# First input projection: sums of products for two pairs of column blocks, and rotary work in earlier steps

## The reference

```python
h = rmsnorm(x, norm_mix[l])
proj = h @ w_in[l]
qa, ka, va, qb, kb, vb, ga, gb = jnp.split(proj, split_points, axis=-1)
qa = rope(rmsnorm(qa.reshape(b, s_len, A_Q_HEADS, HEAD_DIM), a_q_norm[l]), pos)
ka = rope(rmsnorm(ka.reshape(b, s_len, A_KV_HEADS, HEAD_DIM), a_k_norm[l]), pos)
```

## Time and profile before

| | |
|---|---|
| median of 3 runs | 2459.51 us (2459.29 to 2459.89) |
| profiled execution | 2459.43 us |
| its span | 2457.7 us |
| granted TensorE clock, mean | 0.999 |
| TensorE busy | 2445.9 us |
| VectorE busy | 1726.5 us |
| ScalarE busy | 1334.1 us |
| POOL busy | 66.4 us |

### The profile page before, as it was taken

The page is one execution under the profiler, slowest core; times in us unless marked ns, Lnnn a source line. Parts: engine busy times, 40 slices in busy tenths (PEclk is TensorE's granted clock), DMA queues, the critical chain, the costliest instruction groups (busy, mean ns, idle before and its releaser), DMA issues.

```text
span 2457.7 us, 31700 instructions
## 1 busy us (share of the span) xinstructions
PE 2445.9 (100%) x12392; PEld 2072.9 (84%) x12392; DVE 1726.5 (70%) x2077; ACT 1334.1 (54%) x1694; POOL 66.4 (3%) x90
## 2 busy tenths in 40 slices
PE   9999999999999999999999999999999999999998
PEld 7888888888888888888888788888888888888887
DVE  5756767655678777787875457755668779788676
ACT  6444556445555645565555445454656556556453
POOL 0100100000000000000000000000000000000000
PEclk9999999999999999999999999999999999999999
DMA  9655565655555765567557565555565666756663
GB/s 328 206 192 172 164 170 172 224 187 189 189 190 171 244 201 188 188 205 232 181 203 241 163 206 167 163 167 176 171 196 176 220 199 207 220 170 234 216 212 129
DMA packets 256343, 480.98 MB, mean 196 GB/s; under 512 B 23600, under 2 KB 27184, under 8 KB 255584
## 3 DMA queue, kind: packets, MB, share of 16 engines
q1 hardware_dynamic: 251728, 470.98, 57.7%
q0 software_dynamic: 4352, 8.39, 2.0%
q10 hardware_dynamic: 144, 0.03, 0.0%
HBM read 468.85 MB, written 2.13 MB: 192 GB/s over the span
## 4 chain that ended last, share of the span: by engine, by line
PE 98%; DVE 1%; issue 0%; ACT 0%; DMA 0%; DVEq 0%; POOLq 0%; ACTq 0%
PE psum L2364 21%; PE psum L2273 14%; PE psum L2275 14%; PE psum L2274 14%; PE psum L2372 11%; PE psum L2589 4%; PE psum L2591 4%; PE psum L2590 4%; PE psum L2608 2%; PE psum L2609 2%; PE psum L2610 2%; PE psum L2329 1%; PE psum L2334 1%; PE psum L2389 1%; PE psum L2435 0%; DVE wl L1463 0%
## 5 line engine op out<-in xcount | busy, mean ns | idle before, releaser
L1463 DVE TENSOR_TENSOR wl<-raw,wh 128x1024 fp32r<-128x1024 f32 x833 | 1015.3, 1225 | 644.8 <-ACT wh L907 639.8
L907 ACT ACTIVATE wh<-raw 128x1024 fp32r<-128x1024 f32 x833 | 873.3, 1057 | 734.2 <-PE psum L2275 317.1
L2273 PE MATMUL psum<-wh,ha 128*128 128x512 f32 x1248 | 499.4, 400 | 0.7 <-DVE ha L1632 0.7
L2275 PE MATMUL psum<-wh,ha 128*128 128x512 f32 x1248 | 487.1, 390 | 0.0
L2274 PE MATMUL psum<-wl,ha 128*128 128x512 f32 x1248 | 486.5, 390 | 0.0
L2364 PE MATMUL psum<-ha,wh 128*128 128x512 f32 x1344 | 313.1, 390 | 0.0
L2364 PEld LDWEIGHTS psum<-ha,wh 128*128 128x128 f32 x1344 | 249.6, 188 | 50.1
L2275 PEld LDWEIGHTS psum<-wh,ha 128*128 128x128 f32 x1248 | 234.2, 188 | 50.8
L2273 PEld LDWEIGHTS psum<-wh,ha 128*128 128x128 f32 x1248 | 234.6, 188 | 48.3 <-issue 3.3
L2274 PEld LDWEIGHTS psum<-wl,ha 128*128 128x128 f32 x1248 | 234.9, 188 | 44.8
L2364 PE MATMUL psum<-hb,wh 128*128 128x512 f32 x896 | 209.1, 390 | 0.0
(11 more groups left out here) (347 smaller groups left out, 2853.9 us busy)
## 6 DMA issues: line engine op xcount, KB each, us to landing
raw<-in_w_up SPq DMA_DIRECT2D x152, 1024.0 KB, 5.1
raw<-in_w_in SPq DMA_DIRECT2D x116, 1024.0 KB, 5.1
raw<-in_w_down SPq DMA_DIRECT2D x108, 1024.0 KB, 5.1
raw<-in_w_out SPq DMA_DIRECT2D x32, 1024.0 KB, 5.0
raw<-in_w_branch_a SPq DMA_DIRECT2D x8, 1024.0 KB, 5.0
raw<-in_w_branch_b SPq DMA_DIRECT2D x8, 1024.0 KB, 4.9
x_rows<-conv POOLq DMA_DIRECT2D x8, 512.0 KB, 6.6
raw<-in_w_in SPq DMA_DIRECT2D x5, 512.0 KB, 8.0
```

What stands on the lines that cost most here:

```text
L907: act.activation(wh[q % SPLIT_SLOTS][:], src, ACT.Copy).then_inc(hi_done, 1)
L1463: dve.tensor_tensor(wl[q % SPLIT_SLOTS][:], src, wh[q % SPLIT_SLOTS][:].bitcast(F32), ALU.subtract).then_inc(lo_done, 1)
L2273: pe.matmul(acc, hi, wh[s][:, c, :], start=first and c == 0, stop=False)
L2275: ins = pe.matmul(acc, lo, wh[s][:, c, :], start=False, stop=last and c == 1)
```

## The change

Blocks 3 and 4 become a pair, then block 7 runs plainly, blocks 5 and 6 are the second pair, and block 8 runs plainly. In a pair, the weight rows 1024 to 2047 (two of four loads for a block) stay plain, 8 steps of 12 matmuls, and the rows 0 to 1023 become two groups of seven steps of 6 matmuls: 22 steps for 16, and 84 steps for 72 in the stage. The steps of a pair stand in the order of the first 22 steps of `DOWN2_STEPS`, but the sums of the second group begin three steps ahead, not two.

```diff
+IN1_PAIR = [(2, 4), (2, 5), (3, 4), (3, 5)] + seven(1, 0) + [(2, 6), (2, 7)] + seven(1, 1) + [(3, 6), (3, 7)]
+IN1_PAIR_LOADS = [(2, 2), (3, 2), (2, 0), (3, 0), (2, 3), (2, 1), (3, 1), (3, 3)]
+IN1_PAIRS = [(3, 4), (5, 6)]
+S_IN1_PAIR = [24, 24 + len(IN1_PAIR) + 8]
```

VectorE sums the two parts of x and makes four sums for each group in steps 6 and 8, and the low parts of these in steps 7 and 9; ScalarE makes their high parts in its steps 8 and 10, behind its squares of x:

```diff
+            chain.link(dve.tensor_tensor(x_gained[:], both[:, :, 0, :], both[:, :, 1, :], ALU.add))
+            chain.link(dve.tensor_tensor(a_sum0[:, 0], a21, a22, ALU.add))
+            chain.link(dve.tensor_tensor(a_sum0[:, 1], a_sum0[:, 0], a11, ALU.subtract))
+            dve.tensor_tensor(a_sum0[:, 2], a11, a21, ALU.subtract)
+            dve.tensor_tensor(a_sum0[:, 3], a12, a_sum0[:, 1], ALU.subtract).then_inc(sem["x_sums_ok"], 1)
```

The rotary work moves to steps 14 to 37, and the roots on POOL become three instructions of 8 numbers, the mask adds behind the third:

```diff
-            if s == 24:
+            if s == 14:
                 rotation_tables()
...
-            if 26 <= s < 32:
-                if s == 26:
-                    dve.wait_ge(row_free, FREE + 3)
-                piece_sums(s - 26)
...
-            if s in range(36, 54, 3):
-                if s == 36:
-                    dve.wait_ge(sem["an_rs"], 1)
-                piece_rotated((s - 36) // 3)
...
+        piece_steps = {19: 0, 20: 1, 22: 2, 23: 3, 36: 4, 37: 5}
+            if s in (15, 17, 24):
+                i = (15, 17, 24).index(s)
+                dve.wait_ge(row_free, FREE + i + 1)
...
+                piece_sums(2 * i)
+                piece_sums(2 * i + 1)
+                dve.sem_inc(sem["an_ss"], 1)
+            if s in piece_steps:
+                i = piece_steps[s]
+                dve.wait_ge(sem["an_rs"], i // 2 + 1)
+                piece_rotated(i)
+            for i in range(2):
+                n = s - S_IN1_PAIR[i]
+                if 0 <= n < len(IN1_PAIR):
+                    weight_sums(IN1_DOWN + i, n, w_sum0)
+                if 22 <= n < 30:
+                    fold_pair(i, n - 22)
...
-        inverse_root(rsq[:, 0:24], ssq[:, 0:24], 1.0 / HD, 24, sem["an_rs"])
+        for i in range(3):
+            pool.wait_ge(sem["an_ss"], i + 1)
+            inverse_root(rsq[:, 8 * i:8 * i + 8], ssq[:, 8 * i:8 * i + 8], 1.0 / HD, 8, sem["an_rs"])
```

More of the change, by code:

```diff
@@ L59, with seven @@
 T5_BUCKETS = 32
+def seven(pair, group):
+    return [(pair, group, k) for k in range(7)]
+IN1_PAIR = [(2, 4), (2, 5), (3, 4), (3, 5)] + seven(1, 0) + [(2, 6), (2, 7)] + seven(1, 1) + [(3, 6), (3, 7)]
+IN1_PAIR_LOADS = [(2, 2), (3, 2), (2, 0), (3, 0), (2, 3), (2, 1), (3, 1), (3, 3)]
+IN1_PAIRS = [(3, 4), (5, 6)]
+IN1_ORDER = [0, 1, 2, 3, 4, 7, 5, 6, 8]
 S_IN1 = 0
-S_GATE = S_IN1 + 8 * IN1_BLOCKS
+S_IN1_PAIR = [24, 24 + len(IN1_PAIR) + 8]
+L_IN1_PAIR = [12, 12 + 8 + 4]
+S_GATE = S_IN1_PAIR[1] + len(IN1_PAIR) + 8
 S_BRANCH = S_GATE + 8 * GATE_BLOCKS
@@ L84, with early_load @@
 S_IN2 = _s
-L_UP1, L_DOWN1 = [S_FF1 // 2], []
+def early_load(step):
+    extra = len(IN1_PAIR) - 16
+    return (step - extra * sum(step >= s for s in S_IN1_PAIR)) // 2
+L_UP1, L_DOWN1 = [early_load(S_FF1)], []
 for _n in range(2):
@@ L161, in load_done @@
     part = max(p for p in range(3) if p == 0 or u >= L_UP1[p])
-    return (S_UP1[part] if part else 0) + 2 * (u - (L_UP1[part] if part else 0)) + 2
+    if part == 0:
+        return 2 * u + 2 + (len(IN1_PAIR) - 16) * sum(u >= n for n in L_IN1_PAIR)
+    return S_UP1[part] + 2 * (u - L_UP1[part]) + 2
 R_IN1 = 0
@@ L1647, in _, with weight_sum @@
             row_lo(q, 1)
-        for s in range(1, 8 * IN1_BLOCKS):
+        def weight_sum(down, pair, group, n, w_sum):
+            s0, first_load, steps, loads = DOWNS[down]
+            u = first_load + loads.index((2 * pair, group))
+            for v in (u, u + 1):
+                dve.wait_ge(raw_in[v % RAW_SLOTS], 16 * (v // RAW_SLOTS + 1))
+            (b11, b21), (b12, b22) = ([raw[v % RAW_SLOTS][:, 2 * k:2 * k + 2, :] for k in range(2)] for v in (u, u + 1))
+            q = s0 + steps.index((pair, group, 0))
+            made = sums_before(q)
+            if n == 0 and down >= IN1_DOWN and made:
+                dve.wait_ge(lo_done, max(n7 for n7, _, _ in SEVENS if n7 < q) + 7)
+            if n == 2:
+                dve.wait_ge(sem["sum_ok"], made + 1)
+            if n == 3:
+                dve.wait_ge(sem["sum_ok"], made + 3)
+                dve.wait_ge(lo_done, q + 4)
+            plus, minus = ((b12, b11), (b22, b12), (b22, w_sum[0][:]), (b21, w_sum[2][:]))[n]
+            dve.tensor_tensor(w_sum[n % 3][:], plus, minus, ALU.subtract).then_inc(sem["sum_ok"], 1)
@@ new lines, in weight_sums, with x_sums @@
+        def weight_sums(down, s, w_sum):
+            s0, _, steps, _ = DOWNS[down]
+            for n7, step in enumerate(steps):
+                if len(step) == 3 and step[2] == 0:
+                    n = s - sums_begin(steps, step[0], step[1])
+                    if 0 <= n < 4:
+                        weight_sum(down, step[0], step[1], n, w_sum)
+        def x_sums(group):
+            (a11, a12), (a21, a22) = ([x_gained[:, 2 * k:2 * k + 2, P * t:P * t + P] for k in range(2)]
+                                      for t in range(NT))
+            both = ha[:, 4 * group:4 * group + 4, :, :].bitcast(F32)
+            if group:
+                dve.wait_ge(sem["x_sums_hi"], group)
+            chain.link(dve.tensor_tensor(x_gained[:], both[:, :, 0, :], both[:, :, 1, :], ALU.add))
[3 more added lines that the diff above has]
+            dve.tensor_tensor(a_sum0[:, 3], a12, a_sum0[:, 1], ALU.subtract).then_inc(sem["x_sums_ok"], 1)
@@ L1649, in _ @@
+        piece_steps = {19: 0, 20: 1, 22: 2, 23: 3, 36: 4, 37: 5}
+        for s in range(1, S_GATE):
             if s < 5:
@@ L2485, in head_stage, with hb_by, seven_bank, down_banks @@
                 ins.then_inc(sem["at_o"], 1)
+        def hb_by(base, per_count):
+            return lambda j: pe.wait_ge(sem["hb_lo"], base + (2 * j + 1) // 4 + 1)
+        def seven_bank(pair, k):
+            own, shared = 4 * pair, 4 - 4 * pair
+            return (shared, own, own + 2, shared + 1, shared + 3, shared + 2, own + 1)[k]
+        def down_banks(step):
+            if len(step) == 2:
+                return {(step[0] // 2, 2 * step[0] + t) for t in range(NT)}
+            return {(step[0], seven_bank(step[0], step[2]))}
@@ new lines, in down_edges, with down_plain @@
+        def down_edges(steps, s, pair, bank):
+            uses = [n for n, step in enumerate(steps) if (pair, bank) in down_banks(step)]
+            return s == uses[0], s == uses[-1]
+        def down_plain(down, src, acts, s, b, j):
+            q, steps = DOWNS[down][0] + s, DOWNS[down][2]
+            if acts is not None:
+                hb_by(acts, 4)(j)
+            pe.wait_ge(lo_done, q + 1)
+            w = q % SPLIT_SLOTS
+            for c in range(2):
+                for t in range(NT):
+                    acc = psum[:, 2 * b + t, :]
+                    first, last = down_edges(steps, s, b // 2, 2 * b + t)
+                    hi, lo = (src[:, 2 * j + c, part, t * P:(t + 1) * P] for part in range(2))
+                    pe.matmul(acc, hi, wh[w][:, c, :], start=first and c == 0, stop=False)
+                    pe.matmul(acc, hi, wl[w][:, c, :], start=False, stop=False)
+                    ins = pe.matmul(acc, lo, wh[w][:, c, :], start=False, stop=last and c == 1)
+            ins.then_inc(mm_done, 1)
@@ new lines, in down_product @@
+        def down_product(down, src, sums_hi, sums_lo, s, pair, group, k):
+            q, steps = DOWNS[down][0] + s, DOWNS[down][2]
+            pe.wait_ge(lo_done, q + 1)
+            w, bank = q % SPLIT_SLOTS, seven_bank(pair, k)
+            acc = psum[:, bank, :]
+            first, last = down_edges(steps, s, pair, bank)
+            for c in range(2):
+                if k in (0, 1, 6):
+                    t, half = ((0, 0), (0, 1), (1, 1))[(0, 1, 6).index(k)]
+                    hi, lo = (src[:, 4 * group + 2 * half + c, part, P * t:P * t + P] for part in range(2))
+                else:
+                    n = (3, 0, 2, 1)[k - 2]
+                    hi, lo = sums_hi[group][:, n, c, :], sums_lo[group][:, n, c, :]
+                pe.matmul(acc, hi, wh[w][:, c, :], start=first and c == 0, stop=False)
+                pe.matmul(acc, hi, wl[w][:, c, :], start=False, stop=False)
+                ins = pe.matmul(acc, lo, wh[w][:, c, :], start=False, stop=last and c == 1)
+            ins.then_inc(mm_done, 1)
@@ L2573, in down_edges @@
[L2573 to L2592, removed]
```

198 lines of the change are left out of this document (118 added, 80 removed).

## The result

After: 2463.31 us (median of 21 runs, 2462.88 to 2464.90). Before: 2459.51 us (21 runs, 2459.11 to 2459.91). The ratio is 1.0017 [1.0011, 1.0023]: slower, by 3.8 us between the medians, which is clear of no change but less than the 0.2% (4.9 us) set as the bound.

The account below looks back on a forecast made before the run. TensorE bounds the kernel, with VectorE the next limit in groups of seven. Terms -5.4 + 2.0 + 2.5 + 3.1 = +2.2 us on the profiled 2459.43 gave 2461.7 us; range 2457.5 to 2466.0.

Parts of the forecast that it names:

- TensorE, -5.4: First projection: 840 products instead of 864, 24 fewer at 0.2267 us each, all on the path: -5.4 us.
- Sums of x: Steps 6 to 9: VectorE's added sums of x and low parts delay nothing; 0 us, bound 0 to 1.
- First group: Steps 28 to 34, after rotary work: VectorE never idle, step 32's low part late; +2.0 us with restarts, bound 1 to 3.
- Bias adds: POOL's two adds, now amid the first group, take time from VectorE's full queue; +2.5 us, bounds 0 and 2.6.
- Roots: POOL's three roots beside VectorE: 0 by the trace row, about 5.0 us by the skill's rule; the sum took 0.
- Second group: First pair, steps 37 to 43: four sums of weights and two small rotations delay step 41; +3.1 us, bound 2 to 4.
- Second pair, loads, unrolled code: Second pair without rotary work, weight loads, and unrolled code for three engines: 0 us each; bounds to 1, 0.5 and 1.
- the roots hold VectorE too: Slower rival: three POOL roots between steps 15 and 26 delay VectorE, arriving whole at step 32; +5.0, 2466.7 us; chance 0.15.
- the bias adds cost nothing: Rival: POOL waits for a pause or runs after step 32's low part; -0.3 us, 2459.1 us; chance 0.2.
- VectorE keeps pace: Faster rival: less queued between steps 14 and 32, rotations find gaps, the whole 5.4 us stays; 2454.0 us; chance 0.08.

Follow-up runs that it names:

- the version without gaps: Against the kernel after: last four rotations moved to later steps, POOL's bias adds held until the first pair is folded, ScalarE's copy at step 14; 2454.35 us.
- the two-edit version: Against the kernel after: last four rotations moved to later steps and POOL's bias adds held until the first pair is folded, copy left at step 13; 2454.31 us.

## Why the prediction was right, and which term was off

The forecast was 2461.7 us, no difference that can be told: measured 2463.31. The mechanism was the one named, the gain of the products handed back by VectorE, and the gaps stand where the prediction put them: before steps 29 to 32 and 40 to 41, all ended by low parts, none in the second pair. By its steps:

- **TensorE, -5.4:** measured -5.44, and -5.2 net in the version without gaps.
- **Sums of x, 0 (bound 0 to 1): mis-sized.** The run with the copy moved puts 1.3 us on it, more than its bound. The step that failed is "Walked through with ScalarE's order, the low part of step 12 keeps about 0.7 us": that low part did keep its time, but the walk left out the norm's root on POOL and the copy behind it. What the sums of x delayed was not their own low part but ScalarE's squares and POOL's small instructions, and through them the start of step 17's low part, which the next term took at 45.88 "with nothing queued". It began at 47.26.
- **First group, +2.0:** of the 5.55 us of gaps, 2.2 go with the adds and 1.3 with the copy's step; 2.05 are left for the rotary queue, if the parts simply add. With the rotations, the adds and the restarts as counted, the only thing wrong was when the queue began.
- **Bias adds, +2.5 (0 to 2.6):** 2.2 by the stretched rows, and as much by the gaps of the run without them. They began at 84.67, not 81.5, since the last squares came later and the root took 2.49 us, not a third of 5.02, but that is still within the group.
- **Roots, 0 by the row, 5.0 by the rule:** the row was right. The Trainium skill (SBUF — State Buffer, Who interferes with whom) says that a VectorE instruction with two inputs in SBUF contends with a GpSimd instruction that reads SBUF, and that the ports they share are an exclusive lock. For the adds the trace agrees (2.30 us for 1.22). For the roots it doesn't: VectorE lost nothing, while POOL's small instructions waited, 1.29 us for the first of a root, where the one before, begun in a pause of VectorE, took 0.22.
- **Second group, +3.1:** measured 3.05, and 1.6 with one rotation.
- **Second pair, loads, unrolled code, 0:** no gap there, and no gap of after is ended by a load. The load that the prediction gave "about 5.6 us" had cover only because VectorE was late: see the gap behind it in the kernel with the rotations and the adds late. Some 0.45 us of the profiled difference lies outside the counted gaps, 0.2 in remainders within the two groups and 0.25 in later stages; what makes the latter wasn't tried.

The rival "the roots hold VectorE too" gave 2466.7 us and is refuted by the unstretched rows beside a root; "the bias adds cost nothing" by the late adds; "VectorE keeps pace" by the gaps. The last one describes the two-edit version: its 2454.0 us is within 0.4 us of what that measured.

The ends of the range don't follow from the terms that the prediction names for them: without the adds and with the low bound of one group its sum gives about 2458.1, not 2457.5, and with all upper bounds about 2467.2, not 2466.0. The measured time lies inside either.

## What to carry to other kernels

When fewer products make another engine the bound, first list everything that stands in that engine's queue ahead of the dense stretch and on engines that feed it, and move what isn't due there: here four rotations and two adds, none of them due, cost more than the 24 products gave. Work moved ahead of a dense stretch is saved only as far as the relay lets the engine run ahead; if the queue runs empty once on the way, what was saved before that moment is gone. When a sum assumes that a stretch begins "with nothing queued", follow the start itself back through every engine that feeds it.

## What the runs showed of the hardware that was not expected

- Small POOL instructions beside a VectorE that never pauses are held until its running instruction ends: `pairs` took 1.12 us where it had taken 0.20, and `sums` ended at 42.93 where VectorE's row of three low parts had ended at 42.88. In the next pause the third took its usual 0.19. They cost VectorE nothing, while the 128x512 adds took 1.1 us each out of it, with the four rotations in the queue ahead (2.30 and 2.31 us for 1.22) or without (2.31 and 2.32).
- The granted clock fell to 0.50 (1.2 GHz) behind a wait of 2.27 us of TensorE in the profiled executions of two kernels, which cost 1.6 us by the rows; their heaps of runs lie 1.7 to 1.8 us apart. In two other kernels' profiled executions it kept 1.00 behind the same wait. Only kernels with a wait this long have two heaps of runs; those whose longest was 1.71 us, or less, have one. After's own heaps, 1.6 us apart, differ in the mean granted clock of the whole execution: it is 0.999 or 1.0 in all thirteen runs of the lower and 0.998 in seven of the eight of the upper. So the same cause is likely there, though no profile of such a run was taken. In the kernel with one more rotation in the second group the mean doesn't separate them: three of its seven lower runs also show 0.998.
